# First and last RMS norm done by token rows, inside the opening stage and inside the last FFN's stage

## What is computed

```python
def rms_norm(x, w):
    xf = x.astype(F32)
    y = xf * lax.rsqrt(jnp.mean(xf * xf, axis=-1, keepdims=True) + EPS)
    return (y * w.astype(F32)).astype(x.dtype)

# first: n = rms_norm(h, norm1_w), the input of the first mixer
# last:  out = rms_norm(h, the final norm weights of the second part)
```

## Time and profile before

| | |
|---|---|
| runs | 3524.77, 3526.81, 3535.01 us |
| profiled execution, span | 3522.0 us (its own device time stands nowhere apart from these runs; the median run lies 4.8 us above the span) |
| start stage, until the next stage's first matmul | 0 to 24.2 us |
| norm1, until the first matmul of gdn | 24.2 to 38.9 us |
| last copy into the residual in ffn2 | 3492.3 us |
| final_2 and end | 3495.8 to 3522.0 us |
| TensorE busy, ScalarE, VectorE, GpSimd | 92%, 31%, 48%, 7% |

### The profile page before, as it was taken

One profiled execution on the slowest core, in us unless ns is written; L12 is line 12 of the kernel. 1 busy time (PEld: TensorE's weight loads), 2 busy tenths in 40 slices (PEclk: granted clock), 3 DMA queues, 4 the chain that ended last, 5 costly groups with the idle time before them and its releaser, 6 DMA issues. The chain is left out here.

```text
span 3522.0 us, 38723 instructions
## 1 busy us (share of the span) xinstructions
PE 3233.2 (92%) x15292; PEld 2364.5 (67%) x15292; DVE 1688.4 (48%) x2481; ACT 1099.4 (31%) x1673; POOL 248.0 (7%) x193
## 2 busy tenths in 40 slices
PE   6899999878798899999988899999999988899997
PEld 3476576446643478887745688878888764478886
DVE  3757877584400264424467444334432345644423
ACT  3334232262200232212226333223222223632222
POOL 3201200000100110001020100010000011010001
PEclk8999999989799999999999999999999998999998
DMA  2212110342489622222100232223222210022221
GB/s 93 87 61 72 61 49 24 107 145 96 171 319 420 264 96 97 99 99 110 60 7 1 97 107 95 96 72 112 100 98 72 108 66 1 37 84 96 98 100 52
DMA packets 67120, 354.69 MB, mean 101 GB/s; under 512 B 8896, under 2 KB 9408, under 8 KB 29616
## 3 DMA queue, kind: packets, MB, share of 16 engines
q1 hardware_dynamic: 66992, 352.93, 27.2%
HBM read 349.53 MB, written 2.33 MB: 100 GB/s over the span
## 5 line engine op out<-in xcount | busy, mean ns | idle before, releaser
L469 PE MATMUL psum<-next_x_hi,next_w_hi 128*128 128x512 f32 x1408 | 554.0, 393 | 19.2 <-PEq L68 18.2
L469 PE MATMUL psum<-next_x_lo,next_w_hi 128*128 128x512 f32 x1408 | 551.6, 392 | 0.0
L469 PE MATMUL psum<-next_x_hi,next_w_lo 128*128 128x512 f32 x1408 | 551.3, 392 | 0.0
L399 DVE TENSOR_TENSOR next_w_lo<-next_raw,next_w_hi 128x2048 fp32r<-128x2048 f32 x128 | 293.5, 2293 | 455.1 <-ACT next_w_hi L361 455.1
L361 ACT ACTIVATE next_w_hi<-next_raw 128x2048 fp32r<-128x2048 f32 x128 | 245.3, 1916 | 568.9 <-PE psum L469 552.8
L105 PE MATMUL psum<-mix_normed,mix_ring 128*128 128x512 f32 x832 | 363.5, 594 | 9.8 <-ACT recurrences_work L1124 7.1
L469 PEld LDWEIGHTS psum<-next_x_hi,next_w_hi 128*128 128x128 f32 x1408 | 266.8, 190 | 77.4 <-issue 20.7
L469 PEld LDWEIGHTS psum<-next_x_lo,next_w_hi 128*128 128x128 f32 x1408 | 266.7, 189 | 56.3 <-issue 1.0
L469 PEld LDWEIGHTS psum<-next_x_hi,next_w_lo 128*128 128x128 f32 x1408 | 266.6, 189 | 56.2
L105 PEld LDWEIGHTS psum<-mix_normed,mix_ring 128*128 128x128 f32 x832 | 156.1, 190 | 203.8 <-issue 203.2
L469 PE MATMUL psum<-ffn_hid_hi,next_w_hi 128*128 (+1 forms) x704 | 273.9, 389 | 0.0
(11 more groups left out here) (528 smaller groups left out, 5412.6 us busy)
## 6 DMA issues: line engine op xcount, KB each, us to landing
next_raw<-w_ffn SPq DMA_DIRECT2D x128, 1024.0 KB, 4.9
mix_ring<-w_experts SPq DMA_DIRECT2D x48, 1024.0 KB, 13.6
mix_ring<-w_mix SPq DMA_DIRECT2D x32, 1024.0 KB, 7.1
experts_slabs<-w_experts SPq DMA_DIRECT2D x23, 1024.0 KB, 13.8
mix_normed<-w_experts SPq DMA_DIRECT2D x22, 1024.0 KB, 13.7
mix_ring<-w_gdn SPq DMA_DIRECT2D x16, 1024.0 KB, 4.9
mix_ring<-w_ssd SPq DMA_DIRECT2D x10, 1024.0 KB, 5.0
mix_ring<-decay_rows SPq DMA_DIRECT2D x32, 256.0 KB, 5.6
```

The source lines that it names most:

```text
L399: dve.tensor_tensor(w_lo[:, at(q), :], raw[:, at(q), :], w_hi[:, at(q), :].bitcast(F32), ALU.subtract)\
L469: ins = pe.matmul(out, wp[:, at(q), w], xp, start=start and a == 0, stop=stop and a == 2)
```

## The change

The two norm stages and the end stage are removed, and their work is written into the neighbouring stages by token rows. With tokens on partitions the sum of squares of a token is one number of a partition, so root and reciprocal work on columns of 1 or 4 numbers in the new tile `m.stat` instead of on 128x512 tiles.

In the start stage `x` is loaded in four pieces and squared by ScalarE with a running sum (`accum_out`), scaled by VectorE to `scaled_x`, and both `x` and `scaled_x` are transposed: the first gives `m.resid`, the second, times the gain, `m.xT`. VectorE and ScalarE take turns in both sets of copies. GpSimd has nothing to do. In the last ffn2 ScalarE makes, beside each square, a copy of the residual tile times the gain (`m.gained`, in the memory of `next_x_hi`, unused by then). TensorE transposes that while the squares are being added, sums the squares of each token in a column (`m.ps[:, 7, t]`), and the reciprocal root is applied by the copies out of PSUM. The new tile `m.stat` (64 bytes per partition) lies ahead of `norm_tmp`, so that all SBUF buffers behind it move by 64 bytes.

```diff
-def resid_norm_stage(nc, m, name, gain, dst):
...
-def end_stage(nc, m, out):
...
 # ffn_stage, with out=io["out"] in the last layer's ffn2
+    by_token, one = cut(m.stat, 0, NT), m.stat[:, 2 * NT:2 * NT + 1]
...
         @block.sync
+            if out is not None:
+                for t in range(NT):
+                    sp.wait_ge(copied_v, t + 1)
+                    sp.wait_ge(copied_a, t + 1)
+                    sp.dma_start(out[t * P:(t + 1) * P, :], m.by_token[:, t, :]).then_inc(stored, 16)
+                sp.wait_ge(stored, 16 * NT)
...
         @block.scalar
-                square_tiles(act, m, renewed, squared, folded)
+                act.activation(one, m.ones[:, 0:1], ACT.Sqrt)
+                for k in range(KD):
+                    square_tile(act, m, k, renewed, squared, folded)
+                    act.activation(m.gained[:, k, :], m.resid[:, k, :], ACT.Copy, scale=m.gains["final_2"][:, k:k + 1])\
+                        .then_inc(gained, 1)
+                act.wait_ge(token_mean, 1)
+                act.activation(by_token, by_token, ACT.Sqrt).then_inc(token_rooted, 1)
+                act.wait_ge(token_inverted, 1)
+                for t in range(NT):
+                    act.wait_ge(turned, NT + t + 1)
+                    act.activation(m.by_token[:, t, T:D], m.ps[:, NT + t, :], ACT.Copy, scale=by_token[:, t:t + 1])\
+                        .then_inc(copied_a, 1)
...
         @block.vector
+            if out is not None:
+                dve.wait_ge(summed, 2)
+                dve.tensor_scalar(by_token, m.ps[:, 7, 0:NT], 1.0 / D, EPS, ALU.mult, ALU.add).then_inc(token_mean, 1)
+                dve.wait_ge(token_rooted, 1)
+                dve.reciprocal(by_token, by_token).then_inc(token_inverted, 1)
+                dve.wait_ge(token_inverted, 1)
+                for t in range(NT):
+                    dve.wait_ge(turned, t + 1)
+                    dve.tensor_scalar(m.by_token[:, t, 0:T], m.ps[:, t, :], by_token[:, t:t + 1], None, ALU.mult)\
+                        .then_inc(copied_v, 1)
...
         @block.gpsimd
-            fold_squares(pool, m, squared, folded, KD - LATE if hand else KD)
+            fold_squares(pool, m, squared, folded, KD - LATE if hand else KD - 1)
...
         @block.tensor
+            def turn(t, half):
+                for k in range(4):
+                    ins = pe.transpose(m.ps[:, NT * half + t, tok(k)], m.gained[:, 4 * half + k, tok(t)], m.ident)
+                ins.then_inc(turned, 1)
+
             ups_then_downs(pe, up, down, lambda j: down(j, 0, True))
+            if out is not None:
+                pe.wait_ge(gained, 4)
+                for t in range(NT):
+                    turn(t, 0)
+                pe.wait_ge(folded, KD - 2)
+                pe.wait_ge(squared, KD)
+                for t in range(NT):
+                    pe.matmul(m.ps[:, 7, t:t + 1], m.squares[:, tok(t)], m.ones[:, 0:1], start=True, stop=False)
+                    ins = pe.matmul(m.ps[:, 7, t:t + 1], sq_tmp(m, KD - 1)[:, tok(t)], m.ones[:, 0:1], start=False,
+                                    stop=True)
+                ins.then_inc(summed, 1)
+                pe.wait_ge(gained, KD)
+                for t in range(NT):
+                    if t == NT - 1:
+                        pe.wait_ge(token_mean, 1)
+                    turn(t, 1)
...
 def start_stage(nc, m, io):
+    x, scaled_x, junk = cut(m.work, 0, NT, D), cut(m.work, 12 * T, NT, D), cut(m.work, 20 * T, D)
+    by_act = (1, 3, 5, 7)
+    by_dve = (0, 2, 4, 6)
...
         @block.sync
             sp.dma_start(m.const[:, 0:m.rope_at], io["const_f"][:, 0:m.rope_at]).then_inc(const_in, 16)
+            sp.dma_start(m.gain_buf[:, :], io["gains"]).then_inc(const_in, 16)
+            for t in range(NT):
+                sp.dma_start(x[:, t, :], io["x_in"][t * P:(t + 1) * P, :]).then_inc(x_in[t], 16)
             sp.dma_start(m.const[:, behind:], io["const_f"][:, behind:]).then_inc(const_in, 16)
-            sp.dma_start(x, io["x_in"].rearrange("(t p) d -> p t d", p=P)).then_inc(x_in, 16)
-            sp.dma_start(m.gain_buf[:, :], io["gains"]).then_inc(const_in, 16)
...
         @block.tensor
-            pe.wait_ge(const_in, 32)
-            pe.wait_ge(x_in, 16)
+            pe.wait_ge(const_in, 48)
+            for t in range(NT):
+                pe.wait_ge(x_in[t], 16)
+                for k in range(KD):
+                    ins = pe.transpose(m.ps[:, k, tok(t)], x[:, t, tok(k)], m.ident)
+                    if t == NT - 1:
+                        ins.then_inc(turned, 1)
+            pe.wait_ge(scaled, NT)
             for k in range(KD):
+                pe.wait_ge(taken_a if k in by_act else taken_v, k // 2 + 1)
                 for t in range(NT):
-                    ins = pe.transpose(m.ps[:, k, tok(t)], x[:, t, tok(k)], m.ident)
-                ins.then_inc(turned, 1)
+                    ins = pe.transpose(m.ps[:, k, tok(t)], scaled_x[:, t, tok(k)], m.ident)
+                ins.then_inc(gained, 1)
...
         @block.vector
+            for t in range(NT):
+                dve.wait_ge(squared, t + 1)
+                dve.tensor_scalar(rstd[:, t:t + 1], lengths[:, t:t + 1], 1.0 / D, EPS, ALU.mult, ALU.add)\
+                    .then_inc(mean, 1)
+                dve.wait_ge(rooted, t + 1)
+                dve.reciprocal(rstd[:, t:t + 1], rstd[:, t:t + 1]).then_inc(inverted, 1)
+                dve.wait_ge(inverted, t + 1)
+                dve.tensor_scalar(scaled_x[:, t, :], x[:, t, :], rstd[:, t:t + 1], None, ALU.mult).then_inc(scaled, 1)
+            for k in by_dve:
+                take(k)
+            for k in by_dve:
+                dve.wait_ge(gained, k + 1)
+                dve.tensor_scalar(m.xT[:, k, :], m.ps[:, k, :], gain[:, k:k + 1], None, ALU.mult)
...
         @block.scalar
+            for t in range(NT):
+                act.wait_ge(x_in[t], 16)
+                act.activation(junk, x[:, t, :], ACT.Square, accum_out=lengths[:, t:t + 1]).then_inc(squared, 1)
+                act.wait_ge(mean, t + 1)
+                act.activation(rstd[:, t:t + 1], rstd[:, t:t + 1], ACT.Sqrt).then_inc(rooted, 1)
...
 def program(nc, io):
-                    resid_norm_stage(nc, m, "norm1", m.gains["norm1"], m.xT)
...
-        with mixer_memory(nc, m, "out"), work_memory(nc, m, "out", NT * D):
-            resid_norm_stage(nc, m, "final_2", m.gains["final_2"], m.resid)
-            end_stage(nc, m, io["out"])
```

More of the change, by code:

```diff
@@ L118, in columns @@
     return lambda k: w[:, k, half * P:half * P + width]
-def norm_stage(nc, m, name, src, gain, dst, tiles=KD, width=D):
-    with stage(nc, m, name) as (block, sem):
-        squared, summed, rooted, mean, chain = sem(5)
-        rstd = cut(m.norm_tmp, 2 * T, T)
-        @block.scalar
-        def _(act):
-            for k in range(tiles):
-                if k >= 2:
-                    act.wait_ge(summed, k - 1)
-                act.activation(sq[:, k % 2, :], src[:, k, :], ACT.Square).then_inc(squared, 1)
-            act.wait_ge(mean, 1)
-            act.activation(rstd, rstd, ACT.Sqrt).then_inc(rooted, 1)
-        @block.tensor
-        def _(pe):
-            for k in range(tiles):
-                pe.wait_ge(squared, k + 1)
-                pe.matmul(m.ps[:, 0, :], m.ones, sq[:, k % 2, :], start=(k == 0),
-                          stop=(k == tiles - 1)).then_inc(summed, 1)
-        @block.vector
-        def _(dve):
-            dve.wait_ge(summed, tiles)
-            dve.tensor_scalar(rstd, m.ps[:, 0, :], 1.0 / width, EPS, ALU.mult, ALU.add).then_inc(mean, 1)
-            dve.wait_ge(rooted, 1)
-            link = Chain(dve, chain)
-            link(dve.reciprocal(rstd, rstd))
-            for k in range(tiles):
-                dve.scalar_tensor_tensor(dst[:, k, :], src[:, k, :], gain[:, k:k + 1], rstd,
-                                         ALU.mult, ALU.mult)
 def sq_tmp(m, k):
@@ L300, in last_folds, with ffn_stage @@
         pool.tensor_tensor(m.squares, m.squares, cut(m.norm_tmp, (j + 1) % 3 * T, T), ALU.add).then_inc(folded, 1)
-def ffn_stage(nc, m, name, slabs, scale, slot, hand=None, tables=(), settle=False):
+def ffn_stage(nc, m, name, slabs, scale, slot, hand=None, tables=(), settle=False, out=None):
     x_hi, x_lo, w_hi, w_lo, raw = m.x_hi, m.x_lo, m.w_hi, m.w_lo, m.raw
@@ L3196, in layer @@
     else:
-        ffn_stage(nc, m, "ffn2", io["w_ffn2"][l], 0.5, 0)
+        ffn_stage(nc, m, "ffn2", io["w_ffn2"][l], 0.5, 0, out=io["out"])
 def memory(nc, ctx):
@@ L3255, in memory @@
     m.hid_hi, m.hid_lo = (place(f"ffn_hid_{n}", 81920 + 45056 * j, FT, T, dt=F32R) for j, n in enumerate(("hi", "lo")))
+    m.gained = place("final_gained", 0, KD, T)
+    m.by_token = place("final_by_token", 16384, NT, D)
     m.settle_tmp = place("settle_tmp", 147456, 2, T)[:, :, :]
@@ L3430, in start_stage @@
 def start_stage(nc, m, io):
-    x = cut(m.work, 0, NT, D)
-    mask_in = level_masks(m)
```

(15 more changed lines are left out.)

77 lines of the change are left out of this document (10 added, 67 removed).

## The result

| | before | after |
|---|---|---|
| runs | 3525.79 us median of 4 (3520.93 to 3535.01) | 3485.41 us median of 4 (3472.94 to 3497.14) |
| profiled execution, span | 3522.0 | 3471.2 (its own time 3472.94) |
| gdn's first matmul | 38.86 | 21.89 |
| span's end, counted from the end of the last copy into the residual | 29.70 | 12.48 |

The ratio is 0.9885, interval 0.9865 to 0.9905: about 40 us less, where 35.0 were forecast. The two ends came nearly as forecast, so the question is where the rest is from.

A forecast was written before the change was run, and what follows sets the result against it. TensorE was taken as busy almost throughout between gdn and the last ffn2 (92% of the whole span), with waits at both ends. Gains of 17.1 and 17.9 us sum to 35.0: 3526.8 - 35.0 = 3491.8 us, range 3485.5 to 3499.

The forecast's parts named there:

- Term 1: Start stage and removed norm1: gdn's first matmul at 21.8 us instead of 38.86, -17.1 us.
- later than 10.5: Start: the prediction called itself wrong if TensorE started after 10.5 us; it expected 10.0.
- a cost in series: Start loads: roughly 2 us per transfer, three more making 6 us and a start gain of 11; the forecast took 0.
- the clock rival: Half clock in the second transposes ends the start 2 to 3 us later, the end about 1.5; 12 in 100.
- up to 1.2 us: Gdn's first matmuls: possible gain if the short pause ahead of gdn leaves the clock up.
- Term 2: End of the program: span ends at 3504.1 instead of 3522.0, -17.9 us.
- Eight one-column products at 0.12: End: TensorE's sum of squares, priced at 0.12 us per product, ending at 3494.5.
- loads or lengths setting the start: Start: serial load costs or slower squares delay the second transposes to 17 to 20 us, total 3494 to 3498; 8 in 100.
- half of the change doing nothing: Gdn's entry stalls until the old 38.86 us, so only the end's gain remains, 3509; 2 in 100.
- moved buffers slowing the DMA engines: Expert stage: the 64-byte shift lowers DMA throughput, 3549 us at 20% lower; 3 in 100.
- Between gdn and the last ffn2 nothing is changed: Middle of the kernel: TensorE busy there almost throughout, and no gain or loss counted.
- How the numbers follow: Whole kernel: width from copies, hand-overs and run spread (10 us); 3487 to 3496 given 75 in 100.

The follow-up runs named there:

- the 15 copies: Kernel after with 15 chained 128x1024 ScalarE copies ending the start stage, delaying gdn's entry to 38.71 us; ratio 0.9942 to the kernel before.
- the 2 copies: Kernel after with 2 chained 128x1024 ScalarE copies ending the start stage, gdn entered at 24.72 us; a single execution, 3487.24 us.
- the late variant: Kernel after with the end's first 16 transposes moved behind the sum of squares; first store at +7.8 us instead of +4.74, span's end 3.1 later.

## Why the prediction was right, and where it failed

*Start.* Term 1 was -17.1 and measured 21.89 - 38.86 = -17.0, with errors that cancel, so the closeness is in part luck; in the three profiles of the kernel after, gdn was entered at 21.89, 22.17 and 22.39. TensorE began at 11.03, not at 10.0, because the constants behind `x` landed only then, and its first pass ended at 16.3 instead of 15.6; by the prediction's own sign, "later than 10.5", this step was wrong. VectorE's copies and products made up for it: 0.62 and 0.68 us each where 0.73 and 0.77 had been put down, so that its last product ended at 20.71 (forecast 20.7). The second pass took its 3.7. The round of a token length took 1.46 us instead of 1.8, which makes up for pieces of `x` that landed at 5.7, 8.2, 9.5 and 10.7, where 5.6, 7.0, 8.4 and 9.8 had been put down. Whether four pieces cost anything on the queue stays undecided. The late start is below 1.1 us, and the same undivided load varies by 1.5 between kernels; the 6 us of a cost in series are excluded. So the reading in series of what the Trainium skill says in "SBUF — State Buffer", "The DMA setup-cost knee", does not hold for loads queued behind each other here.

*The clock.* The granted clock stayed at 1.00 in the second pass and in the 1.77 us of the barrier, while TensorE did nothing, as the windows of the kernel after show, and in gdn's first sixteen products behind it (21.89 to 28.94, 1.00); before, 21 us with two TensorE records had brought it to 0.50. The first pass is another matter. Its records start 0.21 us apart until 14.3 us and 0.11 apart from there on, in the kernel before as in the kernel after, so it began at half speed; the 1.00 that the first window of the earlier trace rows prints for 10 to 14 us is from before the first change of clock that the profile holds and says nothing. The windows, columns as in the earlier trace rows, after:

```profile
16.43:20.10 3.67, 3.67 (x32) 3.45 (x32) 3.67 (x7) 3.29 (x6) 0.00 (x0) 1.00 0.61 259
20.12:21.89 1.77, 0.00 (x0) 0.03 (x1) 0.59 (x1) 0.69 (x1) 0.02 (x1) 1.00 0.00 0
```

and before:

```profile
17.80:38.80 21.00, 2.05 (x2) 0.50 (x2) 10.34 (x7) 8.58 (x13) 9.98 (x7) 0.50 0.03 11
38.86:47.00 8.14, 8.14 (x16) 2.45 (x16) 0.00 (x0) 0.00 (x0) 2.13 (x3) 0.83 0.02 4
```

The loss of the clock rival did not come, and the gain that it named in passing, "up to 1.2 us", did, with 1.4. With the 15 copies, that is after 18.12 us of idle TensorE, gdn's first sixteen records took 8.83, and with the 2 copies, after 3.99 us, 8.75: the 1.4 go with the short pause ahead of them, not with the new stage as such. At the end the clock rival's price did appear, but in the variants that let TensorE wait ahead of the sum, not in the kernel after.

*End.* Term 2 was -17.9 and measured -17.2. The step "Eight one-column products at 0.12" was mis-sized: an fp32 product is two records, so eight are sixteen, and the sum took 1.94 us instead of 1.0. The first store came at +4.74 instead of +3.8, which is that 0.94. The stores gave 0.26 back. Fold, root and reciprocal, and the copies were as forecast; putting the first 16 transposes ahead of the sum is worth 3.1 us, as the late variant shows, about half of it by the clock.

*Rivals.* The loads or lengths setting the start, half of the change doing nothing, and moved buffers slowing the DMA engines all fell: the first two by rows (entry 21.89, slab products at 28.88 without a wait), the third by the variant with `m.stat` alone. The expert stage, which the third rival would have lengthened, got shorter.

*The middle and the range.* This is what failed. The sum of 35.0 was nearly that of the rows (17.0 + 17.2 = 34.2, and 1.4 in gdn), but the step "Between gdn and the last ffn2 nothing is changed" put the middle at nothing in the sum, and "How the numbers follow" gave it no width either: it took the spread of the runs to be 10 us from three runs, "2 between the lower two". The runs show in its place that the middle is 4.8 +- 0.9 us shorter on the mean, and that executions of one kernel differ by 24 us, with the granted clock. Three measurements of the same kernel gave -40.4, -35.6 and -37.0, on the mean -37.7; the rows of both ends and the mean shift of the middle, 34.2 + 4.8 = 39.0, are among them. Only the first lies outside the range, by 0.1 us, so that the range was missed by the luck of four executions as much as by the shift. What makes the middle's 3.4 us (4.8 less gdn's 1.4) come with the new start stage stays open. The buffers' address and the number of queued loads were tried and are not the cause, and the time of entry is not by the one profile in which it was put back. That the expert stage is shorter, and that it is short when its clock is higher, is what the windows show; what makes the clock so is not shown by any run.

## What to carry to other kernels

Where tokens can be brought onto the partitions, the root and reciprocal of a norm shrink from 128x512 tiles to columns, and the scale can ride on a copy that is made anyway; here this and the barriers that went with it are worth 17 us at each end of the program. Price fp32 matmuls by the records that the trace shows for one, not by instructions. Look where a reordering lets TensorE wait: in the late variant the clock cost about as much as the order. In a long kernel that TensorE bounds, put the spread of executions through the granted clock (3.3 us for each 0.001 here) into the range, even where the change touches only the ends, and don't read a difference between two single profiles as the change's.

## What was not expected of the hardware

- The same first loads end at different times in different profiles: the undivided `x` landed 8.0, 8.1 and 9.5 us after its issue with the old start stage, and 10.1 with the new one.
- Full clock over the pause of 1.77 us without a matmul (1.00 in that window), and 7.05 instead of 8.46 us for the sixteen records behind it; after a pause of 3.99 us they took 8.75.
- A fall of the clock at the end (0.53 in the window behind the sum) after TensorE had waited only 1.83 us and then run sixteen one-column records.
- 24 us between executions of one program, with the clock's mean from 0.962 to 0.969.
- The expert stage has lengths from 327.6 to 335.7 us with the same instructions and, in the thirteen profiles with the new start stage, no fixed one; with the old start stage it kept within 2.1 us.
